# Expert weights loaded in two parts, each after the product that frees its buffer, and the load of expert 3 moved behind two others

## What is computed

```
scores = sigmoid(t @ router_w)              # which group of 4 experts, and which 2 of it
gates  = normalised scores of the chosen two, 0 elsewhere
for e in range(16):
    y = y + gates[:, e:e+1] * ((silu(t @ w1[e]) * (t @ w3[e])) @ w2[e])
x = x + m[5] * y
```

## Time and profile before

| | before |
|---|---|
| median of 3 runs | 885.76 us (885.01 to 886.35) |
| the profiled execution's own time | 883.08 us |
| its span, first to last instruction | 881.3 us |
| TensorE busy | 812.3 us, 92% of the span |
| VectorE / ScalarE / GpSimd busy | 43% / 22% / 13% |
| mean granted TensorE clock | 0.972 of full speed |

### The profile page before, as it was taken

The page is one execution under the profiler, slowest core; times in us unless marked ns, Lnnn a source line. Parts: engine busy times, 40 slices in busy tenths (PEclk is TensorE's granted clock), DMA queues, the critical chain, the costliest instruction groups (busy, mean ns, idle before and its releaser), DMA issues. The chain is left out here.

```text
span 881.3 us, 9675 instructions
## 1 busy us (share of the span) xinstructions
PE 812.3 (92%) x3765; PEld 421.0 (48%) x3765; DVE 380.3 (43%) x841; ACT 193.7 (22%) x404; POOL 112.2 (13%) x101
## 2 busy tenths in 40 slices
PE   4999999999999999999999999999999279999893
PEld 2445465654764544555555555444444134344341
DVE  3229465564346425656567675011124653222211
ACT  4221255200010122322333331010021121122210
POOL 1000000000147510110110111111000102122101
PEclk9999999999999999999999999999999679999997
DMA  8952020300060306234262534720323856799942
GB/s 312 361 205 96 0 96 1 120 2 1 1 232 31 120 3 214 94 108 156 96 199 67 197 111 151 185 96 0 144 95 138 330 224 203 273 375 395 379 124 42
DMA packets 51781, 131.70 MB, mean 149 GB/s; under 512 B 8513, under 2 KB 9234, under 8 KB 47634
## 3 DMA queue, kind: packets, MB, share of 16 engines
q1 hardware_dynamic: 47698, 120.52, 38.2%
q0 software_dynamic: 3456, 8.40, 4.0%
q10 hardware_dynamic: 576, 2.10, 0.6%
HBM read 124.70 MB, written 10.49 MB: 153 GB/s over the span
## 5 line engine op out<-in xcount | busy, mean ns | idle before, releaser
L561 PE MATMUL ps<-arena 128*128 128x512 f32 (+10 forms) x3002 | 730.9, 447 | 22.1 <-issue 5.0
L561 PEld LDWEIGHTS ps<-arena 128*128 128x128 f32 (+5 forms) x3002 | 337.9, 163 | 368.5 <-issue 348.7
L1232 ACT ACTIVATE arena<-ps 128x512 f32<-128x512 f32 (+5 forms) x132 | 55.6, 446 | 215.2 <-PE ps L561 129.7
L564 PE MATMUL ps<-tab,arena 128*128 128x128 f32 x436 | 61.6, 284 | 16.9 <-DMA arena<-xd,tok_of 8.2
L1673 DVE SCALAR_TENSOR_TENSOR arena<-arena,ps 128x512 f32<-128x512 f32 x32 | 22.0, 688 | 119.0 <-ACT arena L1321 118.8
L564 PEld LDWEIGHTS ps<-tab,arena 128*128 128x128 f32 x436 | 51.6, 147 | 44.7 <-issue 30.9
L2174 POOL TENSOR_TENSOR arena<-arena 128x512 f32<-128x512 f32 x24 | 30.5, 1272 | 282.5 <-DVE arena L1673 282.5
L2139 POOL TENSOR_TENSOR stat<-stat,mhalf 128x1 f32<-128x1 f32 (+2 forms) x20 | 23.2, 1162 | 315.7 <-DVE stat L1476 255.8
L1321 ACT ACTIVATE arena<-ps 128x512 f32<-128x512 f32 x32 | 19.1, 598 | 201.6 <-PE ps L561 201.6
L1641 DVE SCALAR_TENSOR_TENSOR arena<-arena,cond 128x512 f32<-128x512 f32 x56 | 42.6, 761 | 2.3 <-PE ps L564 0.6
L1735 DVE TENSOR_REDUCE stat<-ps 128x1 f32<-128x768 f32 (+2 forms) x32 | 27.4, 856 | 24.8 <-PE ps L561 24.3
(11 more groups left out here) (181 smaller groups left out, 371.8 us busy)
## 6 DMA issues: line engine op xcount, KB each, us to landing
arena<-in_moe_w SPq DMA_DIRECT2D x32, 1024.0 KB, 13.7
arena<-in_w_in SPq DMA_DIRECT2D x12, 2048.0 KB, 8.7
arena<-in_mod_w SPq DMA_DIRECT2D x16, 1024.0 KB, 5.1
arena<-in_moe_w SPq DMA_DIRECT2D x32, 512.0 KB, 16.8
arena<-in_mod_w SPq DMA_DIRECT2D x4, 2048.0 KB, 17.0
arena<-in_w_out SPq DMA_DIRECT2D x2, 2048.0 KB, 12.0
arena<-in_x SPq DMA_DIRECT2D x4, 512.0 KB, 5.5
arena<-in_w_in SPq DMA_DIRECT2D x2, 1024.0 KB, 17.9
```

Of the source, the lines that this page charges most:

```text
L561: return nc.tensor.matmul(o, l, r, start=start, stop=stop, skip_group_check=True)
L564: return nc.tensor.transpose(o, i, ident[0:n, 0:n])
L1232: return A_(o, i, ACT.Copy)
```

## The change

First, `load_expert` is divided into `load_hidden` (w1 and w3) and `load_output` (w2). For the ten columns that reuse a buffer, the w1 and w3 of the new expert are issued once `h_mm` says that the `hidden` product of the step that used the buffer is done, and w2 once `y_mm` says so of its `outputs` product. A new list, `LATER_PARTS`, puts these twenty pieces in order: the place of an input piece is `after`, that of an output piece `after + 1.5`. The list comes out as: in 4, in 5, out 4, in 6, in 10, out 5, in 14, in 7, out 6, out 10, in 8, out 14, out 7, in 11, out 8, in 15, out 11, in 9, out 15, out 9. Second, the load of expert 3 moves from before the last tile's store to behind the loads of columns 12 and 13.

```diff
+def later_parts():
+
+    parts = [(after, "in", c, q) for c, q, _, after in LOAD_PLAN if after]
+    parts += [(after + 1.5, "out", c, q) for c, q, _, after in LOAD_PLAN if after]
+    return [(kind, c, q, int(place)) for place, kind, c, q in sorted(parts, key=lambda p: p[0])]
...
-            def load_expert(q, e):
+            def load_hidden(q, e):
                 e = bass.ds(e, 1)
                 sp.dma_start(w13[q][:, 0], A["moe_w1"][0, e].rearrange("e (p k) f -> p (e k) f", k=KD)).then_inc(w13_in[q], 16)
                 sp.dma_start(w13[q][:, 1], A["moe_w3"][0, e].rearrange("e (p k) f -> p (e k) f", k=KD)).then_inc(w13_in[q], 16)
+
+            def load_output(q, e):
+                e = bass.ds(e, 1)
                 for f in range(2):
                     sp.dma_start(w2[q][f], A["moe_w2"][0, e, f * P:(f + 1) * P].rearrange("e p d -> p (e d)")).then_inc(w2_in[q], 16)
...
             for t in range(XT):
                 if t == XT - 1:
-                    for m in range(N_OUT, N_LOADS):
-                        sp.wait_ge(ring_used[m % RING], used_value(m))
-                        load_expert(2 + m - N_OUT, 2 + m - N_OUT)
+                    sp.wait_ge(ring_used[N_OUT % RING], used_value(N_OUT))
+                    load_expert(2, 2)
                 sp.wait_ge(wo_add, 2 * t + 2)
                 sp.dma_start(os[t], xr[:, t]).then_inc(out_done, 16)
...
             for c, q, turn, after in LOAD_PLAN:
-                if c < KNOWN:
+                if c < KNOWN or after:
                     continue
                 if q == SLOTS - 1 and turn == 1:
                     sp.wait_ge(out_done, 16 * XT)
                     sp.wait_ge(xn2_done, XT)
+                load_expert(q, expert_of(c))
+                if q == SLOTS - 1 and turn == 1:
+                    sp.wait_ge(ring_used[(N_OUT + 1) % RING], used_value(N_OUT + 1))
+                    load_expert(3, 3)
+            for kind, c, q, after in LATER_PARTS:
                 e = expert_of(c)
-                if after:
-                    sp.wait_ge(y_mm, after)
-                load_expert(q, e)
+                if kind == "in":
+                    sp.wait_ge(h_mm, after)
+                    load_hidden(q, e)
+                else:
+                    sp.wait_ge(y_mm, after - 1)
+                    load_output(q, e)
```

More of the change, by code:

```diff
@@ L131 @@
 LOAD_PLAN, SLOT_TURNS = load_plan()
+def later_parts():
+    parts = [(after, "in", c, q) for c, q, _, after in LOAD_PLAN if after]
+    parts += [(after + 1.5, "out", c, q) for c, q, _, after in LOAD_PLAN if after]
+    return [(kind, c, q, int(place)) for place, kind, c, q in sorted(parts, key=lambda p: p[0])]
+LATER_PARTS = later_parts()
 SLOT_OF = {c: q for c, q, _, _ in LOAD_PLAN}
@@ L509, in load_expert @@
                 sp.dma_start(w13[q][:, 1], A["moe_w3"][0, e].rearrange("e (p k) f -> p (e k) f", k=KD)).then_inc(w13_in[q], 16)
+            def load_output(q, e):
+                e = bass.ds(e, 1)
                 for f in range(2):
                     sp.dma_start(w2[q][f], A["moe_w2"][0, e, f * P:(f + 1) * P].rearrange("e p d -> p (e d)")).then_inc(w2_in[q], 16)
+            def load_expert(q, e):
+                load_hidden(q, e)
+                load_output(q, e)
             sp.wait_ge(y_copied, NU)
@@ L543, in _ @@
                     sp.wait_ge(xn2_done, XT)
-                e = expert_of(c)
-                if after:
-                    sp.wait_ge(y_mm, after)
-                load_expert(q, e)
+                load_expert(q, expert_of(c))
[3 more added lines that the diff above has]
+            for kind, c, q, after in LATER_PARTS:
+                e = expert_of(c)
+                if kind == "in":
+                    sp.wait_ge(h_mm, after)
+                    load_hidden(q, e)
+                else:
+                    sp.wait_ge(y_mm, after - 1)
+                    load_output(q, e)
             def weights(r):
```

## The result

The changed kernel has a median of 874.9 us (869.74 to 877.89, 4 runs), the kernel before 885.38 us beside it (883.44 to 886.35, 4 runs). The medians differ by 10.5 us or 1.2%; the ratio of all runs is 0.9873, 95% interval 0.9825 to 0.992, so the gain of 1 to 2% is clear of the noise. The profiled execution of the changed kernel took 869.74 us by its own time, 13.3 us less than the 883.08 of before, and is the fastest of its four.

The account below looks back on a forecast made before the run. TensorE, busy 92% of the span, stood still for DMAs before the turn of step 0 and `hidden(10)`. 6.5 + 4.1 + 1.7 - 1.7 = 10.6 us less, from 885.76 to 875.2 us; range 872.3 to 881.0.

Parts of the forecast that it names:

- What held the first gather: Before the turn of step 0: expert 3's load slowed the last `xd` store, delaying the gather; moving it gains 6.5 us.
- The wait before `hidden(10)`: TensorE's wait for column 15's late w3 goes, 4.1 us, and the low clock in `hidden(10)` with it, 1.7 us.
- 25 us to spare: Queue up to column 15's inputs: 35.7 MB end at 804, while `hidden(10)` wants them at some 829.
- over 15 us ahead: Expected sign in the changed profile: column 15's w3 lands over 15 us before `hidden(10)` needs it.
- the 343 GB/s for the weights: Weight rate in the full DMA stretch: eight experts of 3.15 MB in 73.4 us, beside gathers and additions.
- SyncE's issue: SyncE stuck issuing behind a full queue, not ready at `h_mm`: microseconds against 16, eating only slack; no chance of its own.
- The new wait before the turn of step 2: Step 2's gather meets a DMA kept full by expert 3 and column 4; TensorE waits 1.7 us (1.3 to 2.3).
- The clock behind it: After the wait before step 2's turn, TensorE's clock was taken not to fall; 1.7 us as the bound.
- Rival (b): Step 2's gather waits for all queued ahead: 10.9 us lost and 1.7 of clock, 885.8, no change; chance 0.04.

Follow-up runs that it names:

- The experiment with the load behind the store: Kernel before, with expert 3's load issued once the stores to `xd` are in, beside the first gather: 881.4 us, ratio 0.9951.
- the second kernel: Changed kernel with expert 3 loaded at its old place, so only the split of inputs and output matrices: 879.53 us, ratio 0.9922.
- the two partial splits: Kernel before with only columns 11 and 15 split, 882.26 us, or only 4, 5, 6, 10, 14 and 7, 878.87 us; others whole on `y_mm`.
- the first half alone: Kernel before with only expert 3's load moved behind columns 12 and 13, late loads whole on `y_mm`: 879.21 us, ratio 0.9919.

## Why the prediction was right

The forecast was 875.2 us, with 10.6 us of gain by four terms. Both gains came from the places that it named, and the experiments took them apart. That 874.9 meets it within 0.3 us is in part luck: the four runs spread over 8 us, the repeats gave 12.2 and 13.3 us, and one short stretch at the low clock more or less is worth 1.7. By its steps:

- **What held the first gather.** Right in mechanism and size. The store took 2.6 us, the gather was issued at 696.75 (forecast 696.7), took 4.6 us (5.0), and the turn came 6.8 us earlier (6.5). The experiment with the load behind the store shows that both parts of the term are real.
- **The wait before `hidden(10)`.** Right in size: 4.1 us and 1.7 us of clock are gone, and the second kernel, which had them alone, won 6.1 us. The view of it that the prediction gave, release first and bandwidth after, was given its weight by the two partial splits: what pays is the DMA time between 717 and 764 us that lay idle, wholly or in part, and is now used. The step "25 us to spare" was mis-sized, and its sign, w3 of column 15 "over 15 us ahead", failed. In the second trace of the changed kernel that w3, and the start of `hidden(10)`:

```profile
L519 SPq DMA_DIRECT2D arena<-in_moe_w x1: 378/378/378, 793.6 to 793.6; - x1
DMA to landing us min/median/max: 27.8/27.8/27.8
...
832.26 7.09 PE L585 MATMUL ps<-arena 128*64 128x512 f32 x32
```

It landed at 821.4, 10.9 us ahead, and in the third trace 11.0 (822.5 against 833.45). That agrees with the kernel whose inputs came one step, 11.5 us, later and were 0.5 us short; the second kernel, without expert 3 behind 700 us, had 15.9. What was wrong is the 343 GB/s for the weights. I had counted eight experts for the full stretch of before, but column 15's w2 and column 9 stood in the queue behind the w3 that ended it, and the last of them landed only at 850.6. By landings it was six experts and two inputs, 21.0 MB in 73.5 us, or 286 GB/s. In the changed kernel's second trace the 35.7 MB took from 700.6 to 821.4, 296 GB/s. One loss that I had put down as small is SyncE's issue, and it was small: a pair of w2 pieces takes 0.85 us to issue at 731 and at 745 us in the changed kernel, but 3.3 to 3.5 us behind a full queue, and two pairs 8.8 and 12.45, so that a released load is not yet issued. The inputs of column 11 left 2.5 us after their release, the w3 of column 15 2.6 us, out of 16.

- **The new wait before the turn of step 2.** Right in place and cause; a little smaller than the 1.7 us: in the changed kernel's three traces 0.96, 1.57 and 1.44 us, and 1.50 and 1.58 us in the first half alone and in the kernel with inputs one step later. Putting expert 3 later made the gather 4.4 us and the wait vanish.
- **The clock behind it.** Forecast not lost. In the changed kernel's traces it was lost in two of three (waits of 1.44 and 1.57 us) and kept in one (0.96); of the two variants with the same wait one lost it (1.50) and one kept it (1.58). So the term is 1.7 us in three traces of five, and the step "I take no loss of clock" was wrong more often than right.
- **What was not in the sum.** In the profiled execution `outputs(1)` did not run at the low clock after its wait of 2.15 us, 1.7 us that I do not credit to the change: the wait is the same in all twelve traces, and ten of them have 5.37 us, two of the changed kernel's three among them. With the mild new wait and no clock lost behind it, it explains why this execution gained 13.3 us and the median 10.5; the two traces with both stretches at the low clock took 875.64 and 876.58.
- **Rival (b).** Its sum is 0.3 us off: 12.3 us of gains less 10.9 and 1.7 make 886.1 us, not 885.8. The rival fell all the same: in the profiled execution the gather of step 2 took 7.7 us, and no trace waited over 1.6 us for it.

## What to carry to other kernels

A DMA that nobody waits for yet can cost as much as one that is late, when it shares the DMA engines with a small transfer on the path: ask of each bulk load not only when its buffer is free and when it is wanted, but what small store or gather is in flight meanwhile. And where a load lands late behind a full queue, look for idle DMA time further ahead and move the loads that stand before it; freeing the late one alone moves the wait to its neighbour.

## What the runs showed of the hardware

A gather of at most 512 KB took 4.1 to 5.7 us where the DMA engines had time left (shares of 0.24 to 0.84 in the windows of the kernel before and the changed one) and 7.7 to 9.7 us where they were full, however much stood in SyncE's queue: in the kernel before a load issued in the same stretch took 26.7 us. So a gather shares the engines with the bulk load and does not wait behind its backlog. The Trainium skill (DMA: Bandwidth & Descriptors, "Queues, rings and completion order") has each engine go round between the queues with work. The rows agree with that: 8.1 to 8.5 us for gathers beside 26.7 for the load.

TensorE's clock fell from 2.4 to 1.2 GHz for a while after waits as short as 1.44 us (granted clock 0.68 to 0.73 over the stretches behind them, a mean of both levels). It cost 1.7 to 1.8 us each time after waits of 1.44 to 2.15 us, and 1.7 to 2.4 us after waits of about 4.1. In other executions it did not fall after waits of 1.58 and 2.15 us at the same places of the work. The wait of 2.15 us before `outputs(1)` stands in all twelve traces and was followed by the low clock in ten. The two others, one of the changed kernel and the one with inputs a step later, are also those with the shortest `hidden(0)` (9.33 and 9.38 us, the others 9.44 to 9.95); what decides is not shown. Waits of 1.42 and 1.43 us before `hidden(1)` cost no clock in any of the twelve. A short wait has a price that only several traces show.
